# Half-width products in the delta rule's levels, and operand splits moved ahead of three projections, in a one-core fp32 block kernel

## The chip, the cores and the metric

The kernel runs on one core of a Trainium2 chip. The metric is the device time of one execution in microseconds (us), taken as the median of several runs. A core has a matrix engine (PE, with its weight loads shown apart as PEld), a vector engine (DVE), an activation engine (ACT), a general engine (POOL) and a queue engine (SP). In the profile, L532 is line 532 of the kernel.

## The reference, cut to what matters

Two model blocks follow each other over 512 positions of width 2048, in float32. The first ends in a delta rule with 24 value heads, next to a cross attention; its outputs are gated, projected by `w_out` (4096 to 2048) and added to the input. The second block begins with an RMS norm of that sum and one projection whose first tile here holds eight gate columns.

```python
kk = jnp.einsum("bhncd,bhnjd->bhncj", k, k)
m = jnp.where(strict, beta[..., :, None] * kk * decay, 0.0) + jnp.eye(C, dtype=f32)
rhs = jnp.concatenate([v * beta[..., None], k * (beta * jnp.exp(gc))[..., None]], axis=-1)
sol = lax.linalg.triangular_solve(m, rhs, left_side=True, lower=True, unit_diagonal=True)
...
y = jnp.concatenate([mix, xa], axis=-1) * jax.nn.silu(z)
x = x + jnp.einsum("bse,ed->bsd", y, w_out[i])
...
u = rmsnorm(h, norm_w[l])
proj = jnp.einsum('bsd,dc->bsc', u, w_in[l].astype(jnp.float32))
```

## The kernel before, in words

**Projections.** Every weight matrix is a stream of tiles of 2048 x 128. SP loads a tile into `w_raw`, POOL (218 tiles; ACT and DVE do the first 18) splits it into a high part `w_hi` (rounded to fp32r) and the rest `w_lo`. The activations are split the same way into 16 row blocks of `a_hi` (ACT copies) and `a_lo` (DVE subtracts). `gemm` (L386 to L403) issues three matmuls of 512 columns for each of the 16 blocks of a tile: `w_hi` with `a_hi` (L399), `w_hi` with `a_lo` (L400), `w_lo` with `a_hi` (L401). Weights and PSUM have two slots, which the tiles use in turn. A matmul block waits for the semaphore `act_lo` where its operand has only just been split (`fill`).

**Delta rule.** For each of 12 pairs of value heads (index `a`), the 512 positions are four blocks of 128 (index `n`). The triangular inverse of each block grows in levels l = 0 to 6: at level l, a pair of diagonal parts of 2^l columns is joined by one off-diagonal part. Level 0 is a predicated copy alone. At levels 1 to 6 the step `half` computes T1 = N X in bankA (L532), ACT copies bankA to `T1`, and the step `whole` computes the new part of X in bankB (L542, not at the last level) and of its transpose XT in bankC (L544). DVE then writes into X and XT, by `copy_predicated` with the masks `low` and `lowT` (L835), only the elements that the level changes. `NmT`, `X`, `XT` and `T1` are float32, and the trace records each float32 product of the program as two weight loads and two matmuls. `copy_after` and `op` are the helpers by which all DVE instructions go (L835, L829); ACT's go by L1511.

**Order.** `interleave` mixes these steps with the blocks of the tiles of the next pair of heads by a table of weights (`DN_STEPS`). On PE a level is: half(a=0), two gemm blocks, half(a=1), whole(a=0), one gemm block, whole(a=1). All engines walk the same list. `solved` (L551) follows the last level and waits for its copies.

**Around the projection w_out.** Its input has 32 row blocks, handled as two halves of 16. The first 16 tiles (W_OUT + 0 to 15) take the outputs of the first eight head pairs, the next 16 (W_OUT + KT + ...) those of the other four and of the cross attention (`ys`). The outputs lie in DRAM (`y_dram`); `load_early` brings two blocks at a time into a ring of three buffers (`y_rows`), `early_high` and `early_low` split them. `AHEAD` = 4 of the blocks are split before the steps of the last head pair begin, the other 12 are split between these steps, as their gemm block comes up. At the second half, `high(3, ...)` and `fill(3, ...)` split all 16 blocks of `ys` once the last tile of the first half is finished, since `a_hi` and `a_lo` are read until then. The same holds for `high(4, ...)` and `fill(4, ...)` ahead of the gate tile W_GATE. There the norm's sum of squares (`run_sum`, L627) is computed first.

Of the kernel before, what the change touches and what calls it, by code (L numbers as in the profile page):

```python
# [26 lines left out]
P = 128  # L27
T = 512
# [108 lines left out]
AHEAD = 4  # L137
# [26 lines left out]
def build(nc, weights, xT, memT, peT, params, consts, out):  # L164
# [8 lines left out]
    with ctx:  # L173
# [113 lines left out]

        def quad(bank):
            return bank[:, :, :].rearrange("p a (n t) -> p a n t", n=NB)
# [13 lines left out]
        names = ("src_loaded mem_in par_loaded x_made act_hi act_lo squared sq_summed root_ready "  # L303
# [16 lines left out]
        def gains(c, n=1):  # L320
            return par[:, c:c + n]

# [22 lines left out]
        def _(sp):  # L345
# [3 lines left out]
            with sp.Fori(0, (W_END + 1) // 2 - 1) as i:  # L349
                for w in range(2):  # L350
# [3 lines left out]
                        "a p k c -> p (a k) c")).then_inc(raw_loaded[w], 16)  # L354
            for w in range(2):
                sp.wait_ge(raw_loaded[w], 16 * ((W_END + 1) // 2))
# [30 lines left out]
        def _(pe):  # L387
            def gemm(base, c, k, fill=None, i=0, per=0, width=T):
# [13 lines left out]
                if k == KT - 1:  # L402
                    last.then_inc(gemm_done[slot], 1)  # L403

# [93 lines left out]
            def dn_mix(step, j):  # L498
# [25 lines left out]
                elif step[0] == "half":  # L524
# [86 lines left out]
            with pe.Fori(0, (KT - EARLY) // 2) as i:  # L611
                for c in range(2):
                    for k in range(KT):
                        gemm(W_OUT + EARLY, c, k, None, i, 2)
            for k in range(KT):
# [3 lines left out]
            with pe.Fori(0, KT // 2 - 1) as i:  # L619
                for c in range(2):  # L620
                    for k in range(KT):
                        gemm(W_OUT + KT + 2, c, k, None, i, 2)

# [7 lines left out]
            run_sum(2)  # L631
            for k in range(KT):
                gemm(W_GATE, 0, k, 4)

# [188 lines left out]
        def _(v):  # L823
# [189 lines left out]
            def dn_mix(step, j, g=None):  # L1013
# [31 lines left out]
                elif step[0] == "whole":  # L1045
                    l, a = step[1:3]
                    v.wait_ge(s["dd"], level_count(j, l, a))
                    if l < LEVELS - 1:
                        copy_after(v.copy_predicated, X[:, a, :, :], low[:, l:l + 1, :].to_broadcast([P, NB, P]),
                                   quad(bankB)[:, a, :, :])  # L1050
                    copy_after(v.copy_predicated, XT[:, a, :, :], lowT[:, l:l + 1, :].to_broadcast([P, NB, P]),
# [1107 lines left out]
```

## Time and profile before

| what | value |
|---|---|
| median of three runs | 3446.03 us (3445.16 to 3446.71) |
| the profiled execution's own time | 3445.93 us |
| its span, first to last instruction | 3444.1 us |
| mean granted clock of PE | 0.989 of full |
| busy share: PE, PEld | 96%, 80% |
| busy share: DVE, ACT, POOL | 45%, 25%, 49% |

The profile shows one execution. Busy time of PE is the union of overlapping matmuls, so it says that PE had something in flight, and not that each matmul came as fast as it can. The distance from one matmul's start to the next is read from the timeline: a merged row of n equal matmuls is (n - 1) distances and one duration long. Idle time of an engine counts only where PE later waits for it.

### The profile page before, as it was taken

The numbers are of one execution on the slowest core, as the hardware profiler recorded it, in microseconds if no ns is written. First come the engines' busy times: TensorE is split into PE (matmuls) and PEld (weight loads), VectorE is DVE, ScalarE is ACT, GpSimd is POOL, SyncE is SP. The second block draws the span as 40 slices with busy tenths as digits, with TensorE's granted clock in tenths as the row PEclk, the third lists the DMA queues.
The fourth block names the chain that finished last, engine by engine and source line by source line (L and its number), as shares of the span: only waits on it lengthen the run. The fifth ranks groups of instructions, "written<-read, shape, count | busy, mean of one in ns | idle before, by whom it ended". The sixth has DMA issues, their size and how long they took to land.

```text
span 3444.1 us, 47302 instructions
## 1 busy us (share of the span) xinstructions
PE 3302.3 (96%) x17232; PEld 2768.1 (80%) x17232; DVE 1534.9 (45%) x2049; ACT 864.2 (25%) x1291; POOL 1698.4 (49%) x1748
## 2 busy tenths in 40 slices
PE   8999999999999999999899999999998999999996
PEld 7877888888888888888688787777777878778685
DVE  6722245444544454445431213343455665631723
ACT  5411133322332233223310102111113232310411
POOL 0255634433443344334326676656665555556774
PEclk9999999999999999999999999999999999999998
DMA  6322212111211121112214223222223222223222
GB/s 237 125 90 85 95 41 85 61 55 56 84 62 53 57 83 62 54 59 81 97 68 171 86 98 134 94 90 91 97 91 121 76 79 76 88 98 122 74 98 85
DMA packets 53529, 306.51 MB, mean 89 GB/s; under 512 B 5044, under 2 KB 7220, under 8 KB 21716
## 3 DMA queue, kind: packets, MB, share of 16 engines
q1 hardware_dynamic: 33984, 247.48, 21.0%
q10 hardware_dynamic: 19476, 58.05, 4.5%
q8 instruction: 50, 0.82, 0.1%
q14 instruction: 19, 0.16, 0.0%
HBM read 284.74 MB, written 20.77 MB: 89 GB/s over the span
## 4 chain that ended last, share of the span: by engine, by line
PE 82%; DVE 11%; ACT 4%; issue 2%; DMA 1%; ACTq 0%; DVEq 0%
PE gemm_ps L399 19%; PE gemm_ps L401 19%; PE gemm_ps L400 19%; DVE arena L829 9%; PE bankC L544 4%; PE bankB L542 3%; PE bankA L532 3%; ACT arena L1511 2%; PE gemm_ps L746 2%; PE gemm_ps L748 2%; PE gemm_ps L747 2%; PE bankA L702 2%; DVE a_lo L829 1%; ACT a_hi L1511 1%; DVE arena L835 1%
## 5 line engine op out<-in xcount | busy, mean ns | idle before, releaser
L399 PE MATMUL gemm_ps<-a_hi,w_hi 128*128 128x512 f32 (+1 forms) x3472 | 1385.5, 399 | 33.7 <-DVE a_lo L829 28.8
L375 POOL CAST w_hi<-w_raw 128x512 fp32r<-128x512 f32 x872 | 548.6, 671 | 1698.9 <-issue 1541.3
L401 PE MATMUL gemm_ps<-a_hi,w_lo 128*128 128x512 f32 (+1 forms) x3472 | 1332.5, 384 | 0.0
L400 PE MATMUL gemm_ps<-a_lo,w_hi 128*128 128x512 f32 (+1 forms) x3472 | 1330.5, 383 | 0.0
L367 POOL TENSOR_TENSOR w_lo<-w_raw,w_hi 128x512 fp32r<-128x512 f32 x872 | 1153.6, 1354 | 4.2
L399 PEld LDWEIGHTS gemm_ps<-a_hi,w_hi 128*128 128x128 f32 x3472 | 657.6, 189 | 169.2 <-issue 28.2
L401 PEld LDWEIGHTS gemm_ps<-a_hi,w_lo 128*128 128x128 f32 x3472 | 655.7, 189 | 130.9
L400 PEld LDWEIGHTS gemm_ps<-a_lo,w_hi 128*128 128x128 f32 x3472 | 658.0, 190 | 121.7 <-issue 8.4
L829 DVE TENSOR_TENSOR arena<-gemm_ps,arena 128x512 f32<-128x512 f32 (+3 forms) x161 | 107.1, 665 | 633.0 <-PE gemm_ps L401 514.1
L829 DVE RECIPROCAL arena<-arena 128x512 f32<-128x512 f32 (+2 forms) x70 | 172.8, 2468 | 321.3 <-ACT arena L1511 319.1
L1511 ACT ACTIVATE arena<-arena 128x512 f32<-128x512 f32 (+5 forms) x350 | 214.8, 614 | 398.9 <-DVE arena L829 384.5
L829 DVE TENSOR_TENSOR arena<-arena 128x512 f32<-128x512 f32 (+4 forms) x219 | 212.7, 971 | 52.6 <-ACT arena L1801 28.9
L544 PE MATMUL bankC<-arena 128*128 128x128 f32 x1152 | 210.9, 275 | 0.0
L542 PE MATMUL bankB<-arena 128*128 128x128 f32 x960 | 186.1, 275 | 12.3 <-DVE arena L829 12.3
L1511 ACT ACTIVATE arena<-bankA 128x512 f32<-128x512 f32 x144 | 86.1, 598 | 391.6 <-PE bankA L532 391.4
L835 DVE COPY_PREDICATED arena<-con,bankB 128x512 f32<-128x512 uint32 x120 | 88.1, 734 | 202.6 <-PE bankC L544 200.9
L1511 ACT ACT_TABLE_LOAD x104 | 133.4, 1283 | 170.6 <-DVE arena L829 123.5
L544 PEld LDWEIGHTS bankC<-arena 128*128 128x128 f32 x1152 | 170.0, 192 | 1.0
L542 PEld LDWEIGHTS bankB<-arena 128*128 128x128 f32 x960 | 150.0, 191 | 19.3 <-ACT arena L1511 11.9
L829 DVE SCALAR_TENSOR_TENSOR arena<-gemm_ps,arena 128x511 f32<-128x511 f32 x144 | 107.8, 749 | 126.5 <-ACT arena L1511 123.2
L532 PE MATMUL bankA<-arena 128*128 128x128 f32 x1152 | 152.1, 275 | 0.6 <-ACT arena L1511 0.6
L532 PEld LDWEIGHTS bankA<-arena 128*128 128x128 f32 x1152 | 146.2, 191 | 7.5 <-ACT arena L1511 1.0
(162 smaller groups left out, 2679.2 us busy)
## 6 DMA issues: line engine op xcount, KB each, us to landing
w_raw<-w_stream SPq DMA_DIRECT2D x236, 1024.0 KB, 4.9
y_scratch<-arena ACTq DMA_DIRECT2D x20, 512.0 KB, 3.4
arena<-y_scratch ACTq DMA_DIRECT2D x15, 512.0 KB, 4.1
arena<-gc_scratch ACTq DMA_DIRECT2D x12, 512.0 KB, 3.6
arena<-x_t ACTq DMA_DIRECT2D x2, 2048.0 KB, 10.2
arena<-y_scratch ACTq DMA_DIRECT2D x1, 4096.0 KB, 25.2
x_scratch<-arena ACTq DMA_DIRECT2D x1, 4096.0 KB, 12.1
y_out<-arena ACTq DMA_DIRECT2D x4, 1024.0 KB, 3.9
```

The costliest lines, as they stand in the source:

```text
L367: return pool.tensor_tensor(part(w_lo, w, q), part(w_raw, w, q), part(w_hi, w, q).bitcast(F32), ALU.subtract)
L375: pool.tensor_copy(part(w_hi, w, q), part(w_raw, w, q)).then_inc(pool_step, 1)
L399: pe.matmul(o, hi, a_hi[:, k, 0:width], start=(k == 0), stop=False)
L400: pe.matmul(o, hi, a_lo[:, k, 0:width], start=False, stop=False)
L401: last = pe.matmul(o, lo, a_hi[:, k, 0:width], start=False, stop=(k == KT - 1))
L532: last = pe.matmul(quad(bankA)[:, a, n, :], NmT[:, a, n, :], X[:, a, n, :], start=True, stop=True)
L542: pe.matmul(quad(bankB)[:, a, n, :], XT[:, a, n, :], T1[:, a, n, :], start=True, stop=True)
L544: last = pe.matmul(quad(bankC)[:, a, n, :], T1[:, a, n, :], XT[:, a, n, :], start=True, stop=True)
L702: last = pe.matmul(bankA[:, l % 2, b], w[:, b], w[:, b], start=True, stop=True)
L829: d.did(make(*args), sem, value)
L835: d.did(make(*args), sem, value)
L1511: d.did(act.activation(dst, src, func, **kw), sem, value)
```

## The change

The products of a level are issued for 64 of the 128 columns: T1 and the new part of X for the columns of the first half of each pair, the new part of XT for those of the second half. They are written packed into the first 64 columns per block of the PSUM bank (`half_chunk`), and the operand read is strided (`half_columns`). ACT's copy into T1 and DVE's predicated copies handle 256 elements a partition instead of 512. T1 is cleared once before the first head pair.

Ahead of the three projections the splits are moved. `AHEAD` becomes 16: all blocks of the first half are split before the last head pair's steps. The loads of their first four blocks move from ACT's queue to SP's, some tiles earlier. For the second half and for the gate tile, the last tile ahead is taken out of PE's loop and signals each of its blocks by the new semaphore `block_free`; ACT and DVE split block k as soon as that tile has passed it. `run_sum(2)` moves from before the gate tile to after its 13th block.

```diff
-AHEAD = 4
+AHEAD = KT
...
+        def half_chunk(bank, a, n):
+            return bank[:, a, n * (P // 2):(n + 1) * (P // 2)]
...
+        def half_columns(x, l, second):
+            h = 1 << l
+            return x.rearrange("p (b t) -> p b t", t=2 * h)[:, :, h * second:h * second + h]
...
+            asked = W_OUT // 2 - 2
+            with sp.Fori(0, asked) as i:
+                pair_of_tiles(i)
+            sp.wait_ge(s["dy_stored"], 16 * 3)
+            for p in range(2):
+                sp.dma_start(y_rows(p), y_dram[2 * p:2 * p + 2].rearrange("a p t -> p a t")).then_inc(
+                    s[f"early_y{p}"], 16)
...
                     for n in range(NB):
-                        last = pe.matmul(quad(bankA)[:, a, n, :], NmT[:, a, n, :], X[:, a, n, :],
-                                         start=True, stop=True)
+                        last = pe.matmul(half_chunk(bankA, a, n), NmT[:, a, n, :],
+                                         half_columns(X[:, a, n, :], l, 0), start=True, stop=True)
...
-                            pe.matmul(quad(bankB)[:, a, n, :], XT[:, a, n, :], T1[:, a, n, :],
-                                      start=True, stop=True)
-                        last = pe.matmul(quad(bankC)[:, a, n, :], T1[:, a, n, :], XT[:, a, n, :],
-                                         start=True, stop=True)
+                            pe.matmul(half_chunk(bankB, a, n), XT[:, a, n, :],
+                                      half_columns(T1[:, a, n, :], l, 0), start=True, stop=True)
+                        last = pe.matmul(half_chunk(bankC, a, n), T1[:, a, n, :],
+                                         half_columns(XT[:, a, n, :], l, 1), start=True, stop=True)
...
-            pe.wait_ge(s["o_root"], 2 * QKH)
-            run_sum(2)
             for k in range(KT):
                 gemm(W_GATE, 0, k, 4)
+                if k == KT - 4:
+                    run_sum(2)
...
-                        copy_after(v.copy_predicated, X[:, a, :, :], low[:, l:l + 1, :].to_broadcast([P, NB, P]),
-                                   quad(bankB)[:, a, :, :])
+                        copy_after(v.copy_predicated, level_blocks(chunks(X, a), l, 0), level_mask(low, l, 0),
+                                   by_level(half_bank(bankB, a), l))
...
+            add_tile(xt[:, KT - 2, :], W_OUT + KT - 2, 0)
             v.wait_ge(s["ys_loaded"], 16)
-            fill(3, ys, None)
+            for k in range(12):
+                low_block(3, k, ys)
+            add_tile(xt[:, KT - 1, :], W_OUT + KT - 2, 1)
+            for k in range(12, KT):
+                low_block(3, k, ys)
...
-            fill(4, xt, C_NORM2)
+            add_tile(xt[:, KT - 2, :], W_OUT + 2 * KT - 2, 0, q=2, row=KT - 2)
+            for k in range(12):
+                low_block(4, k, xt, C_NORM2)
+            add_tile(xt[:, KT - 1, :], W_OUT + 2 * KT - 2, 1, q=2, row=KT - 1)
+            for k in range(12, KT):
+                low_block(4, k, xt, C_NORM2)
...
-                    op(T1[:, a, :, :], quad(bankA)[:, a, :, :], ACT.Copy, s["t1_sbuf"], level_count(j, l, a))
+                    op(half_columns(chunks(T1, a), l, 0), half_bank(bankA, a).rearrange("p (b t) -> p b t", t=1 << l),
+                       ACT.Copy, s["t1_sbuf"], level_count(j, l, a))
...
+            def high_block(f, base, k, src, gain=None):
+                slot, n = tile_at(base, KT - 1)
+                if k < KT - 1:
+                    act.wait_ge(s["block_free"], (KT - 1) * (f - 3) + k + 1)
+                else:
+                    act.wait_ge(gemm_done[slot], n + 1)
+                op(a_hi[:, k, :], src[:, k, :], ACT.Copy, act_hi, CUT_AT[f] + k + 1,
+                   scale=1.0 if gain is None else gains(gain + k))
```

On DVE, at the start of the last head pair, the rows before are these. `a_lo<-arena,a_hi` is the split of one block; the copy from `con` begins the step `natural`.

```order
L829 TENSOR_TENSOR a_lo<-arena,a_hi 128x512 [waits dy_ready]
L829 TENSOR_TENSOR a_lo<-arena,a_hi 128x512 [waits act_lo,act_hi] x3
L829 COPY arena<-con 128x1024 [waits act_lo]
L829 RECIPROCAL arena<-arena 128x4 [waits dve_step,k_root]
L829 TENSOR_TENSOR arena<-arena 128x8 [waits dve_step] x2
L829 SCALAR_TENSOR_TENSOR arena<-bankA,arena 128x128 [waits dve_step,expd,pair]
L829 SCALAR_TENSOR_TENSOR arena<-bankA,arena 128x128 [waits dve_step] x7
L835 COPY_PREDICATED arena<-con,arena 128x1024 [waits dve_step]
...
L829 TENSOR_TENSOR a_lo<-arena,a_hi 128x512 [waits pm_ready,act_hi]
L829 TENSOR_TENSOR a_lo<-arena,a_hi 128x512 [waits act_lo,act_hi] x11
```

And these are the same place's rows in the changed kernel:

```order
L879 TENSOR_TENSOR a_lo<-arena,a_hi 128x512 [waits dy_ready]
L879 TENSOR_TENSOR a_lo<-arena,a_hi 128x512 [waits act_lo,act_hi] x15
L879 COPY arena<-con 128x1024 [waits act_lo]
L879 RECIPROCAL arena<-arena 128x4 [waits dve_step,k_root]
L879 TENSOR_TENSOR arena<-arena 128x8 [waits dve_step] x2
L879 SCALAR_TENSOR_TENSOR arena<-bankA,arena 128x128 [waits dve_step,expd,pair]
L879 SCALAR_TENSOR_TENSOR arena<-bankA,arena 128x128 [waits dve_step] x7
L885 COPY_PREDICATED arena<-con,arena 128x1024 [waits dve_step]
```

The 12 splits that stood behind the step now stand ahead of it; ACT's list has its 12 copies to `a_hi` moved in the same way.

On DVE, ahead of the gate tile, the rows before are these (the end of the loop over tiles, then the splits, then the norm's reciprocal):

```order
L829 TENSOR_TENSOR arena<-gemm_ps,arena 128x512
L1117 REGISTER_ALU
L829 TENSOR_TENSOR arena<-arena 128x512 [waits evicted0,sq_run]
L1155 REGISTER_ALU
L1155 COMPARE_AND_BRANCH
L95 ISA [waits act_hi,gemm_done1,gemm_done0]
L829 SCALAR_TENSOR_TENSOR a_lo<-arena,par,a_hi 128x512 [waits sq_acc]
L829 SCALAR_TENSOR_TENSOR a_lo<-arena,par,a_hi 128x512 [waits act_lo,act_hi] x15
L829 RECIPROCAL arena<-arena 128x512 [waits act_lo,root_ready]
```

In the changed kernel they are:

```order
L879 TENSOR_TENSOR arena<-gemm_ps,arena 128x512 [waits sq_acc]
L879 TENSOR_TENSOR arena<-arena 128x512 [waits evicted1,sq_run]
L879 SCALAR_TENSOR_TENSOR a_lo<-arena,par,a_hi 128x512 [waits sq_acc,act_hi]
L879 SCALAR_TENSOR_TENSOR a_lo<-arena,par,a_hi 128x512 [waits act_lo,act_hi] x11
L879 TENSOR_TENSOR arena<-gemm_ps,arena 128x512 [waits act_lo,gemm_done0]
L879 TENSOR_TENSOR arena<-arena 128x512 [waits evicted0,sq_run]
L879 SCALAR_TENSOR_TENSOR a_lo<-arena,par,a_hi 128x512 [waits sq_acc,act_hi]
L879 SCALAR_TENSOR_TENSOR a_lo<-arena,par,a_hi 128x512 [waits act_lo,act_hi] x3
L879 RECIPROCAL arena<-arena 128x512 [waits act_lo,root_ready]
```

Twelve of the sixteen splits now stand ahead of the addition that empties the last tile's PSUM slot and of its square; the same pattern, without the square, stands at the second half of `w_out`.

## Rows read from the trace of the kernel before

**Rows 1.** The page: the chain that ended last, by engine.

```profile
PE 82%; DVE 11%; ACT 4%; issue 2%; DMA 1%; ACTq 0%; DVEq 0%
```

**Rows 2.** Groups by form: the levels' products (count, busy us, mean ns).

```profile
L544 PE MATMUL bankC<-arena 128*128 128x128 f32 x1152 | 210.9, 275 | 0.0
L542 PE MATMUL bankB<-arena 128*128 128x128 f32 x960 | 186.1, 275 | 12.3 <-DVE arena L829 12.3
L532 PE MATMUL bankA<-arena 128*128 128x128 f32 x1152 | 152.1, 275 | 0.6 <-ACT arena L1511 0.6
```

**Rows 3.** Timeline of PE (start us, us): products, transposes, transposes of four columns.

```profile
701.18 1.06 PE L532 MATMUL bankA<-arena 128*128 128x128 f32 x8
...
1724.73 1.04 PE L515 MATMUL bankC<-con,arena 128*128 128x128 f32 x8
...
2239.97 0.41 PE L678 MATMUL bankB<-con,arena 4*128 4x4 f32 x4
```

**Rows 4.** Lines L532 and L522 (transposes): duration ns, min/median/max.

```profile
L532 PEld LDWEIGHTS bankA<-arena x1152: 186/192/192, 454.6 to 1781.5; 128*128 128x128 f32 x192
L532 PE MATMUL bankA<-arena x1152: 270/275/377, 454.6 to 1781.6; 128*128 128x128 f32 x192
...
L522 PE MATMUL bankC<-con,arena x96: 272/273/328, 448.9 to 1737.2; 128*128 128x128 f32 x96
```

**Rows 5.** Timeline at the end of a head pair's levels, and a strided form.

```profile
614.46 2.28 PE L551 MATMUL bankA<-arena 128*128 128x128 f32 x16
...
614.80 0.73 DVE L835 COPY_PREDICATED arena<-con,bankC 128x512 f32<-128x512 uint32 x1 [0.85 <-PE bankC L544]
...
L829 DVE TENSOR_TENSOR bankB<-bankC,arena 128x256 f32<-128x256 f32 x48 | 20.8, 432 | 1.6
```

**Rows 6.** Timeline and chain of waits around the last head pair's start.

```profile
1698.50 0.39 PE L508 MATMUL bankA<-arena 128*128 128x128 f32 x2
...
1700.09 3.60 DMA arena<-y_scratch
...
1706.31 0.37 ACTq L1750 DMA_DIRECT2D arena<-y_scratch  x1
...
1707.45 0.69 DVE L829 TENSOR_TENSOR a_lo<-arena,a_hi 128x512 fp32r<-128x512 f32 x1 [0.43 <-ACT a_hi L1511]
...
1712.83 0.63 ACT L1511 ACTIVATE a_hi<-arena 128x512 fp32r<-128x512 f32 x1 [1.32 <-DMA arena<-y_scratch]
...
1713.36 1.29 DVE L835 COPY_PREDICATED arena<-con,arena 128x1024 f32<-128x1024 uint32 x1 [0.16 <-DVE arena L829]
...
1736.47 1.04 PE L522 MATMUL bankC<-con,arena 128*128 128x128 f32 x8
```

**Rows 7.** Timeline of DVE: the tiles' additions around the second half's start.

```profile
1943.51 0.69 DVE L829 TENSOR_TENSOR arena<-gemm_ps,arena 128x512 f32 x1 [10.17 <-PE gemm_ps L401]
...
1962.62 0.69 DVE L829 TENSOR_TENSOR arena<-gemm_ps,arena 128x512 f32<-128x512 f32 x1 [1.07 <-PE gemm_ps L401]
```

**Rows 8.** Groups by form: splits beside POOL's (1947 to 1954) and alone (to 1961.8).

```profile
L829 DVE TENSOR_TENSOR a_lo<-arena,a_hi 128x512 fp32r<-128x512 f32 x5 | 7.3, 1454 | 0.5
...
L367 POOL TENSOR_TENSOR w_lo<-w_raw,w_hi 128x512 fp32r<-128x512 f32 x4 | 6.7, 1709 | 0.0
...
L829 DVE TENSOR_TENSOR a_lo<-arena,a_hi 128x512 fp32r<-128x512 f32 x9 | 6.2, 692 | 1.3 <-DVE a_lo L829 0.5
```

**Rows 9.** Timeline of PE around the gate tile, and after it.

```profile
2125.42 0.39 PE L401 MATMUL gemm_ps<-a_hi,w_lo 128*128 128x512 f32 x1
...
2147.58 0.40 PE L399 MATMUL gemm_ps<-a_hi,w_hi 128*128 128x512 f32 x1
...
2172.86 0.47 PE L399 MATMUL gemm_ps<-a_hi,w_hi 128*128 128x512 f32 x1 [3.34 <-DVE arena L829]
```

**Rows 10.** Stretches: PE busy (instructions), granted clock, DMA share, GB/s.

```profile
1945.00:1955.00 10.00, 6.70 (x21) 1.00 0.09 13
1710.00:1720.00 10.00, 1.91 (x6) 0.63 0.26 88
```

More of the change, by code:

```diff
@@ L321, in gains, with level_mask, by_level, level_blocks @@
             return par[:, c:c + n]
+        def half_columns(x, l, second):
+            h = 1 << l
+            return x.rearrange("p (b t) -> p b t", t=2 * h)[:, :, h * second:h * second + h]
+        def level_mask(mask, l, second):
+            h = 1 << l
+            m = half_columns(mask[:, l, :], l, second)
+            return m[:, None, :, :].to_broadcast([P, NB, P // (2 * h), h])
+        def by_level(x, l):
+            return x.rearrange("p (n b t) -> p n b t", n=NB, t=1 << l)
+        def level_blocks(x, l, second):
+            h = 1 << l
+            return x.rearrange("p (n b t) -> p n b t", n=NB, t=2 * h)[:, :, :, h * second:h * second + h]
+        def chunks(x, a):
+            return x[:, a, :, :].rearrange("p n t -> p (n t)")
         def level_count(j, l, a):
@@ L403, in gemm @@
                     last.then_inc(gemm_done[slot], 1)
+                elif frees:
+                    last.then_inc(s["block_free"], 1)
             def memory_sum(k):
@@ L614, in _ @@
                         gemm(W_OUT + EARLY, c, k, None, i, 2)
+            for c in range(2):
+                for k in range(KT):
+                    gemm(W_OUT + KT - 2, c, k, frees=(c == 1))
             for k in range(KT):
@@ L622, in _ @@
                         gemm(W_OUT + KT + 2, c, k, None, i, 2)
+            for c in range(2):
+                for k in range(KT):
+                    gemm(W_OUT + 2 * KT - 2, c, k, frees=(c == 1))
             def run_sum(q):
@@ L1097, in _ @@
             v.wait_ge(s["y_stored"], 16 * XH)
+            op(v.memset, T1[:, :, :, :], 0.0)
             v.sem_inc(s["o_root"], 2)
@@ L1111, in add_tile @@
                 if q is not None:
-                    add_squares(q, c if per == 0 else 2 * i + 2 + c, c)
+                    add_squares(q, row if row is not None else c if per == 0 else 2 * i + 2 + c, c)
             def add_squares(q, k, c):
@@ L1761, in early_high @@
                     load_early(p + 2)
-            act.wait_ge(s["dy_stored"], 16 * QKH)
-            for p in range(3):
-                if p == 2:
-                    act.wait_ge(s["gate"], QKH)
-                load_early(p)
+            act.wait_ge(s["gate"], QKH)
+            load_early(2)
             for w in range(2):
@@ L1790, in _ @@
             act.wait_ge(s["ys_loaded"], 16)
-            high(3, ys)
+            def high_block(f, base, k, src, gain=None):
+                slot, n = tile_at(base, KT - 1)
+                if k < KT - 1:
+                    act.wait_ge(s["block_free"], (KT - 1) * (f - 3) + k + 1)
+                else:
+                    act.wait_ge(gemm_done[slot], n + 1)
+                op(a_hi[:, k, :], src[:, k, :], ACT.Copy, act_hi, CUT_AT[f] + k + 1,
+                   scale=1.0 if gain is None else gains(gain + k))
+            for k in range(KT):
+                high_block(3, W_OUT, k, ys)
             def run_square(q, k, c):
@@ L1814, in run_squares @@
                         one(2 * i + 2 + c, c, *tile_at(base + 2, c, i, 2))
-                d.leave(KT // 2 - 1)
+                d.leave(KT // 2 - 2)
+                one(KT - 2, 0, *tile_at(base, KT - 2))
+                if q == 2:
+                    for k in range(KT - 2):
+                        high_block(4, W_OUT + KT, k, xt, C_NORM2)
+                one(KT - 1, 1, *tile_at(base, KT - 1))
+                if q == 2:
+                    for k in range(KT - 2, KT):
+                        high_block(4, W_OUT + KT, k, xt, C_NORM2)
             def run_root(q):
@@ L1827, in _ @@
             run_root(2)
-            high(4, xt, gain=C_NORM2)
             act.wait_ge(s["h_lb"], 1)
```

38 lines of the change are left out of this document (25 added, 13 removed).

## The prediction

> **What bounds the kernel now.** I read the page first, then the waits of PE, then the timeline where PE waits. PE is the bound: the chain that ended last runs over it for 82% [rows 1], and the page has it busy 96% of the span. So two questions decide: does a level's product come sooner, and how much of PE's waiting goes. For the first the reader is to look at the distance between products, not at their duration, since they overlap. Eight recorded products of 128 columns take 1.06 us with one duration of 275 ns in it, so one comes every (1060 - 275) / 7 = 112 ns [rows 2 and 3]. For the second, PE has three long waits around the two halves of `w_out` and the gate tile; within the head pairs it hardly waits.
>
> **Products of the levels.** 1152 + 960 + 1152 = 3264 recorded products [rows 2] go from 128 to 64 moving columns. Their weights stay 128 x 128 (`NmT`, `XT`, `T1`). What a product waits for is then the question: its columns, or its weight load.
>
> Columns: transposes move 128 columns too, and come every (1040 - 273) / 7 = 109.6 ns [rows 3 and 4]. The products come every 112 ns, slightly later than the same columns need, so something else already ends last. Loads: a product that finds PE empty takes 377 ns, a transpose that finds it empty 328 ns, at equal columns [rows 4]. The 49 ns are the longer load of a float32 product. Four transposes of only four columns take 0.41 us with one duration of at least 0.2 us in it, about 0.07 us each [rows 3]: with next to nothing to stream, the short load and its overhead set that distance. The long load then sets at most 70 + 49 = 119 ns, and the same sum without the few ns of swapping (61 + 49, from the closest distance that the four allow) gives 110. The observed 112 lies between. I conclude that the products are bound by their weight loads already, and that half the columns bring nothing: 3264 x 0 = 0. Bounds: at best the step falls to 107 ns (3264 x -5 ns = -16 us), at worst two ns are added by the packed writes (+7 us). I take 0, as the row of the products is itself the nearest.
>
> The Trainium skill weighs in on both sides. "TensorE: Matmul & The Clock Gate", section "LDWEIGHTS (loading the stationary operand)", puts a load of P columns at P / 1.2 ns, whatever the moving side does: 107 ns for 128, which speaks against this part of the change; the trace agrees within 5 ns. The same page's "Back-to-back issue gap" prices a lone matmul by its moving columns only; by that rule the step would halve, which is the first rival below.
>
> **ACT's and DVE's copies.** DVE's copies fall from 0.73 us to about 0.43 (a strided form of 256 elements takes 432 ns), ACT's likewise [rows 5]. Nearly all of it lies beside PE. The exception is the end of each head pair: the 16 products of `solved` take 2.28 us, where 15 x 0.112 + 0.275 = 1.95 would do. PE waits for the last copy (start 614.80, 0.73 long) and refills [rows 5]. With a copy of 0.43 us it is done before the first eight products are (614.46 + 0.90 = 615.36). That is 12 x 0.33 = -4 us (bounds -4 and 0). The wait at level 1 of each head pair, 12.3 us in all [rows 2], hangs on DVE's steps ahead of the levels and stays. The clearing of T1 lies beside a tile of PE: 0.
>
> **The first half's splits.** Before: PE ends the products of the last pair's first step at 1698.9 and reaches the transposes of XT at 1736.5 [rows 6]. Between lie 18 gemm blocks and 8 transposes. A tile takes 10.17 + 0.69 = 10.86 us [rows 7], a block 0.68, so that is 12.2 + 0.9 = 13.1 us of work in 37.6: 24.5 us lost. After: SP has loaded four blocks long before, so ACT begins at about 1700.3 and not at 1703.9, as the load's 3.60 us goes from the path [rows 6]. The other 12 blocks come two at a time through three buffers. A buffer is reloaded when DVE has split it, and a load takes 3.6 to 6.5 us (issued 1706.31, used 1712.83 [rows 6]). With about 4.2, and 2.4 for the splits, a pair of blocks comes each 6.6 / 3 = 2.2 us. DVE's first four end near 1706, two of them beside POOL; the last ends at 1706 + 6 x 2.2 = 1719. Then the step `natural`, now queued behind all 16 splits, runs: from the last split to XT's mask copy was 1714.65 - 1708.14 = 6.5 us [rows 6]. PE reaches the transposes at 1725.6: -10.9 us. It has then waited 5 us in front of them, and after such a wait the granted clock fell (0.63 over 1710 to 1720 [rows 10], after an idle of 8 us); I put 2 us for it. Sum: -9. Bounds: -13 if the loads keep to 3.6 us, -4 if each takes 6.5. The two loads that move to SP stand ahead of a weight tile, whose buffer POOL needs only a tile later: 0.
>
> **The second half's splits.** Before, the additions of two neighbouring tiles start at 1943.51 and 1962.62, 19.11 us apart instead of 10.86 [rows 7]: 8.2 us lost. After, DVE starts 1.4 us into the last tile of the first half (one addition, one block of PE). What is late next is DVE itself, as it has now to split beside POOL. A split takes 0.69 us alone and 1.45 beside POOL (mean of five), and POOL's subtractions take 1.71 then, one split to each [rows 8]. POOL is busy 49% of the span for 218 tiles, 7.8 us a tile, and more while DVE is in its way. Going through it instruction by instruction (steps of 1.7 us beside POOL's subtractions, 1.0 beside its casts, 0.8 alone), split 12 ends at 16.5 us, the addition at 17.2, the last split at 23.1. PE wants the last block at 10.9 + 15 x 0.68 = 21.1. So 2 us are lost: -8.2 + 2 = -6. Bounds: -8 (DVE in time), -4 (all at 1.7).
>
> **The gate tile.** From the last matmul ahead (2125.4 + 0.2) to the next tile's first (2147.6) [rows 9] are 21.9 us for a tile of 10.9 and the norm's two products, 0.9: 10.2 lost. After, the same race, with a square and its addition in between for which DVE waits 0.8 us, and splits of 0.86 us alone: split 12 ends at 18.9, split 13 at 23.1, and PE wants block 13 at 19.1. That is a wait of 4 us: -10.2 + 4 = -6. Bounds: -10, and -3 if the clock falls in that wait. The norm's root comes as late as the last split, and DVE's work from there to the wait of 3.34 us at 2172.86 [rows 9] is the same and starts equally late: 0 (-3 to +2).
>
> **Sum.** 0 - 4 - 9 - 6 - 6 = -25 us. The profiled execution took 3445.93 us, span 3444.1 and 1.8 around it, and the median is 3446.03, so nothing has to be shifted: 3421 us. The terms' bounds add up to 3393 and 3443.
>
> **Rivals.**
> *Products bound by their columns.* The load is hidden, and the step goes to half of 107 plus 5 ns, or to the 61 to 70 of the four-column transposes [rows 3]: 3264 x -46 ns = -150 us, in all 3270. For it: the 112 ns lie close to what 128 columns need, and only 2.4 ns separate the two readings. Against: the 49 ns between the two kinds at equal columns [rows 4], which must be on the load's side. Chance 0.07.
> *Strided reads, the side of slower.* PE reads its 64 columns in runs of 2 to 64 elements; before, all its operands are contiguous. If a read in short runs takes four times as long, the step is 213 ns: at all levels 3264 x 101 ns = +330, in all 3750; at level 1 alone (576 products) +58, 3479. It decides from a mean step of 112 + 25 / 3.264 = 120 ns on. For it: no row shows a strided read by PE; DVE reads such runs at full speed (432 ns for 256 elements [rows 5]). Chance 0.05.
> "SBUF — State Buffer", section "Door 1: The DMA port swizzle", of the Trainium skill says that two accesses to a line of 16 bytes suffice for full speed; the shortest run here is two float32. No run here shows it.
> *Clock.* Half as many columns in flight could let the granted clock fall within the levels. Each us at half clock costs half a us, so 50 us of it eat the gain; all levels at half clock would cost 12 x 44 us. Against: from 1945 to 1955, PE ran 21 matmuls of L399 to L401's kind in 10 us, less dense than a level will be, at clock 1.00 [rows 10]. Chance 0.02.
> *The moved splits only trade waits.* DVE and POOL hold each other up more than I reckon, the loads stay at 6.5 us: the lower bounds of all three, 3435. This is inside my own case.
>
> **How the numbers follow.** My case has 0.86. Within it 3405 to 3434 holds most. A run can tell 0.2%, 7 us: of the 0.86, 0.03 fall within it and 0.01 beyond on the slow side. Faster: 0.82 + 0.07 = 0.89. Same 0.03. Slower 0.01 + 0.05 + 0.02 = 0.08. The range 3400 to 3438 leaves out the fast rival, the slow ones and some of each tail.
>
> **What would show it.** Right: merged rows of eight level products with a step of 110 to 113 ns, and durations of about 222 ns (275 less 53); the row of L551's successor at 1.95 us for 16; the head pairs' trips 0.3 us shorter and not 12; the transposes of XT some 11 us earlier; additions at the second half 13 us apart; a wait near block 13 of the gate tile; DVE's splits at 1.5 us and more beside POOL. Wrong: a step near 60 ns (first rival), one above 120 at level 1 (second), granted clock below 1.00 between 455 and 1690 (third), or a DVE copy with short runs above 0.73 us, which PE would wait for at every level.

## The result and the profile after

The changed kernel takes 3466.3 us (median of 4 runs, 3465.6 to 3470.4) against 3446.4 (4 runs, 3445.2 to 3446.8). The ratio is 1.0061, with a 95% interval of 1.0047 to 1.0075: slower by 0.6%, 20 us. Forecast were 3421 us and 3400 to 3438. The profiled execution took 3470.4 us, its span is 3468.6.

The page, read first, shows little of it: PE is busy 96% of the span and holds 83% of the chain, where it held 82% [rows 1]. One figure does point the way: the mean granted clock is 0.976, where it was 0.989. The groups by form answer to [rows 2]:

```profile
L587 PE MATMUL bankC<-arena 128*128 128x64 f32 x1152 | 221.2, 285 | 0.0
L585 PE MATMUL bankB<-arena 128*128 128x64 f32 x960 | 192.7, 284 | 11.0 <-DVE arena L879 10.5 <-ACT arena L1580 0.5
L575 PE MATMUL bankA<-arena 128*128 128x64 f32 x1152 | 160.1, 286 | 1.6 <-ACT arena L1580 1.6
```

Half the columns, and the mean duration rose from 275 to 285 ns. The line of the first product tells why; these are minimum, median and maximum:

```profile
L575 PEld LDWEIGHTS bankA<-arena x1152: 186/192/338, 456.1 to 1818.2; 128*128 128x128 f32 x192
L575 PE MATMUL bankA<-arena x1152: 217/275/421, 456.1 to 1818.3; 128*128 128x64 f32 x192
```

The median stayed; some take 421 ns, and their weight loads 338. The timeline of PE at the second head pair's first levels shows where:

```profile
571.50 1.00 PE L575 MATMUL bankA<-arena 128*128 128x64 f32 x8
572.31 0.48 PE L440 MATMUL gemm_ps<-a_hi,w_hi 128*128 128x512 f32 x1
...
573.78 1.00 PE L575 MATMUL bankA<-arena 128*128 128x64 f32 x8
575.87 0.41 PE L585 MATMUL bankB<-arena 128*128 128x64 f32 x2 [1.09 <-DVE arena L879]
...
583.19 1.91 PE L575 MATMUL bankA<-arena 128*128 128x64 f32 x8
...
587.32 1.00 PE L575 MATMUL bankA<-arena 128*128 128x64 f32 x8
```

Eight products take 1.00 us, then 1.91, then 1.00 again. At full clock the second product of such a row starts 58 ns after the first, where that distance was 108 ns before; it is the one place where fewer columns show. The other six distances are 112 ns, as before: 0.058 + 6 x 0.112 + 0.272 for the last duration = 1.00. The 50 ns do not reach the time either, since the gemm behind starts 0.81 us after the row's start (572.31 - 571.50) as it did before (571.18 - 570.37, below). In the slow row the step is (1.91 - 0.42) / 7 = 213 ns. That is a clock, so the stretches have to be read with the granted clock (length, busy us and instructions of PE, PEld, DVE, ACT, POOL, then the clock). The first and last stretch are the second and seventh pair's, at the same place of their levels, the middle one the sixth pair's:

```profile
576.80:587.00 10.20, 10.20 (x42) 9.52 (x42) 2.92 (x4) 0.38 (x1) 0.00 (x0) 0.50 0.18 74
1054.70:1078.50 23.80, 23.80 (x98) 22.25 (x97) 5.20 (x10) 1.84 (x4) 1.39 (x3) 0.50 0.01 6
1178.80:1189.00 10.20, 10.20 (x81) 9.69 (x81) 3.82 (x6) 0.78 (x2) 0.00 (x0) 1.00 0.17 71
```

Busy share cannot show it: PE is busy 10.20 of 10.20 us in the first and the last, but does 42 instructions in one and 81 in the other. Half clock (1.2 GHz) begins 5 to 7 us after the first level product in eight of twelve pairs and lasts 10.2 us, in one of them 23.9 (the first pair has 3.4 us of it, which cost its trip nothing); in the kernel before no pair's levels have any. The first level products of neighbouring pairs give what it costs:

```profile
690.64 1.00 PE L575 MATMUL bankA<-arena 128*128 128x64 f32 x8
...
1173.50 1.00 PE L575 MATMUL bankA<-arena 128*128 128x64 f32 x8
...
1287.82 1.00 PE L575 MATMUL bankA<-arena 128*128 128x64 f32 x8
```

A trip with the drop takes 690.64 - 571.50 = 119.1 us, one without 1287.82 - 1173.50 = 114.3. So a drop costs 4.8 us, and the long one, of the pair that starts at 1047.94, 11.2 (1173.50 - 1047.94 - 114.3). Before, the trips were 114.65 (685.03 - 570.37):

```profile
570.37 1.05 PE L532 MATMUL bankA<-arena 128*128 128x128 f32 x8
571.18 0.48 PE L399 MATMUL gemm_ps<-a_hi,w_hi 128*128 128x512 f32 x1
...
685.03 1.05 PE L532 MATMUL bankA<-arena 128*128 128x128 f32 x8
```

Both kernels issue the same gemms and products in the same order, up to the norm's two products in the gate tile. So each matmul of one trace can be set against the same of the other, and the lag tells where time went: +1.4 us before the levels, 7 x 4.80 + 11.25 = +44.9 by the clock in the pairs, -3.8 by shorter trips (11 x 0.35), -5.9 in the first half, -6.0 in the second, -5.8 in the gate tile and the tile behind it. The sum is +24.8; the profiled executions differ by 24.5. That is 4 us more than the medians do, as the profiled execution was the slowest of the four.

### The profile page after: what moved, and what is told of

It reads as the page before. It is cut to its first block, busy times and chain, and to the rows that moved or that the text cites. A ratio compares the mean times of both kernels' runs of the same rounds, so it can differ in the third digit from the quotient of the medians.

```text
span 3468.6 us, 47303 instructions
## 1 busy us (share of the span) xinstructions
PE 3343.5 (96%) x17232; PEld 2811.5 (81%) x17232; DVE 1484.1 (43%) x2050; ACT 833.5 (24%) x1291; POOL 1704.9 (49%) x1748
## 4 chain that ended last, share of the span: by engine, by line
PE 83%; DVE 11%; ACT 3%; issue 2%; DMA 1%; ACTq 0%; DVEq 0%
PE gemm_ps L440 19%; PE gemm_ps L442 19%; PE gemm_ps L441 19%; DVE arena L879 8%; PE bankC L587 4%; PE bankA L575 3%; PE bankB L585 3%; PE gemm_ps L796 2%; ACT arena L1580 2%; DVE a_lo L879 2%; PE gemm_ps L798 2%; PE gemm_ps L797 2%; PE bankA L752 2%; PE bankA L594 1%; PE bankB L599 1%
## 5 line engine op out<-in xcount | busy, mean ns | idle before, releaser
L587 PE MATMUL bankC<-arena 128*128 128x64 f32 x1152 | 221.2, 285 | 0.0
L585 PE MATMUL bankB<-arena 128*128 128x64 f32 x960 | 192.7, 284 | 11.0 <-DVE arena L879 10.5
L587 PEld LDWEIGHTS bankC<-arena 128*128 128x128 f32 x1152 | 180.9, 203 | 1.1
L885 DVE COPY_PREDICATED arena<-con,bankB 128x256 f32<-128x256 uint32 x120 | 59.7, 498 | 284.1 <-PE bankC L587 282.7
L585 PEld LDWEIGHTS bankB<-arena 128*128 128x128 f32 x960 | 161.2, 205 | 18.3 <-ACT arena L1580 12.2
L575 PEld LDWEIGHTS bankA<-arena 128*128 128x128 f32 x1152 | 160.1, 207 | 10.0 <-ACT arena L1580 2.0
L1580 ACT ACTIVATE arena<-bankA 128x256 f32<-128x256 f32 x144 | 55.9, 388 | 457.9 <-PE bankA L575 457.8
L575 PE MATMUL bankA<-arena 128*128 128x64 f32 x1152 | 160.1, 286 | 1.6 <-ACT arena L1580 1.6
```

The lines of the kernel that those rows point to most:

```text
L575: last = pe.matmul(half_chunk(bankA, a, n), NmT[:, a, n, :], half_columns(X[:, a, n, :], l, 0), start=True, stop=True)
L585: pe.matmul(half_chunk(bankB, a, n), XT[:, a, n, :], half_columns(T1[:, a, n, :], l, 0), start=True, stop=True)
L587: last = pe.matmul(half_chunk(bankC, a, n), T1[:, a, n, :], half_columns(XT[:, a, n, :], l, 1), start=True, stop=True)
L1580: d.did(act.activation(dst, src, func, **kw), sem, value)
```

## The experiments

The theory to test (A): the 64-column products let the clock fall at the first levels, with the wait of 1.1 us in front of level 1's second products, and all else went about as forecast. The rivals: the moved splits and loads disturb the levels (B); the short runs of columns do, in DVE's and ACT's copies (C) or in PE's reads.

**The change without the levels.** Products and copies as before, splits moved:

```diff
-                        last = pe.matmul(half_chunk(bankA, a, n), NmT[:, a, n, :],
-                                         half_columns(X[:, a, n, :], l, 0), start=True, stop=True)
+                        last = pe.matmul(quad(bankA)[:, a, n, :], NmT[:, a, n, :], X[:, a, n, :],
+                                         start=True, stop=True)
...
```

> The changed kernel with the levels as they were before (products and both kinds of copies over 128 columns, T1 not cleared); only the splits of the two halves of w_out and of the gate tile stay moved. Theory A (the 64-column products let the granted clock fall at each head pair's first levels, and that is all that the change lost): no half clock within the head pairs (456 to 1690 us), trips of 114.6 us, time 3446 - 18 (5.8 + 7.7 + 4.1, what the changed trace gained at the three places) = 3428, perhaps down to 3422 if the half clock after the first half goes too. Theory B (the moved splits and loads disturb the levels): the trips stay at 119.1 us and the time at 3466. Theory C (DVE's and ACT's copies in short runs make the loss): as A for this kernel.

Measured: 3431.0 us, ratio 0.9954 (0.9936 to 0.9971). No half clock in the pairs, trips 114.65. B fell.

**The levels alone**, on the kernel before:

```diff
-                    op(T1[:, a, :, :], quad(bankA)[:, a, :, :], ACT.Copy, s["t1_sbuf"], level_count(j, l, a))
+                    op(half_columns(chunks(T1, a), l, 0), half_bank(bankA, a).rearrange("p (b t) -> p b t", t=1 << l),
+                       ACT.Copy, s["t1_sbuf"], level_count(j, l, a))
...
```

> The kernel before with the level change alone (64-column products, narrowed copies, T1 cleared); splits and loads where they were. Theory A: half clock in most head pairs, 5 to 7 us after the pair's first product; trips of 119 us where it falls and 114.3 where not; time 3446 + 42 = 3488. Theory B: no half clock in the pairs, trips 114.3, time 3443. Theory C: as A for the time, but with gaps in PE's stream instead of a lower clock.

Measured: 3473.7 us (3464 to 3499), ratio 1.007 (1.005 to 1.009). Half clock in eight pairs, as in the changed kernel, in two of them 23.9 us long; trips 119.1 and 114.3. The loss comes with the levels alone. 3488 was too exact: the time varies by 34 us between executions, and the mean granted clock with it, from 0.982 in the fastest to 0.972 in the slowest, which is the one that the trace shows.

**Level 1 wide.** 128 columns in level 1's products only:

```diff
+                        if not (l == 1):
...
+                        else:
+                            last = pe.matmul(quad(bankA)[:, a, n, :], NmT[:, a, n, :], X[:, a, n, :],
+                                             start=True, stop=True)
...
```

> The changed kernel with 128-column products at level 1 alone (their copies stay narrow and read the banks in runs); levels 2 to 6 keep 64 columns. Theory A1 (it is the few columns together with the wait of 1.1 us in front of level 1's second products): no half clock within the pairs, trips of 114.3 us, time 3466 - 42 = 3424. Theory A2 (64 columns alone are too few, at any level): half clock comes at level 2 or 3 of each pair instead, trips stay at 119, time about 3466. The strided-read theory with the shortest runs as the cause would give 3424 too; it is told apart by the contiguous kernel of this call.

Measured: 3427.4 us, ratio 0.9942 (0.9923 to 0.9962), trips 114.3, no half clock in the pairs. The second pair, at the same place as above:

```profile
576.50:586.70 10.20, 10.20 (x82) 9.68 (x80) 3.81 (x6) 0.77 (x2) 0.00 (x0) 1.00 0.17 73
```

Level 2 and the rest run on 64 columns at full clock. So narrow products at levels 2 to 6 are not enough; it needs those of level 1.

**Contiguous columns.**

```diff
-                                         half_columns(X[:, a, n, :], l, 0), start=True, stop=True)
+                                         X[:, a, n, 0:P // 2], start=True, stop=True)
...
```

> The changed kernel whose 64-column products read 64 contiguous columns (the first 64 of X and T1, the last 64 of XT) instead of the columns of their level, so that the levels do not compute the inverse; counts, shapes, weights and all copies are the same. Theory A (width): half clock in the pairs as in the changed kernel, step 112 ns at full clock, time 3466 within 5. Strided-read theory (short runs upset PE's stream or its clock): no half clock, trips 114.3, time 3424.

Measured: 3462.2 us (10 runs, 3448.9 to 3475.4), ratio 1.0047 (1.0030 to 1.0064). Half clock in seven of the pairs, at +5.3 to +6.4 us, trips 119.1 with and 114.3 without. Its second pair:

```profile
576.70:586.90 10.20, 10.20 (x42) 9.52 (x41) 2.92 (x4) 0.38 (x1) 0.00 (x0) 0.50 0.18 74
```

The runs of columns are not the cause; the width is.

**No wait, 64 columns.** If level 1 matters because PE also waits there, filling that wait must keep the clock up:

```diff
-               for s, a, w in (("half", 0, 2), ("half", 1, 0), ("whole", 0, 1), ("whole", 1, 0))]
+               for s, a, w in (("half", 0, 2), ("half", 1, 2 if l == 1 else 0), ("whole", 0, 1), ("whole", 1, 0))]
...
-            + [("head_out", 28)])
+            + [("head_out", 26)])
```

> The changed kernel, 64 columns at every level, with two gemm blocks (1.36 us) moved from the end of each head pair's trip to between the second `half` and the first `whole` of level 1, so that PE has work in place of its wait of 1.1 us for kd_ready. Theory A1 (few columns and the wait together bring the clock down): no half clock in the pairs, trips of 114.3 - 1.1 = 113.2 us, time 3466 - 42 - 12 = 3412. Theory A2 (64 columns are too few by themselves): half clock stays in most pairs, trips near 118, time about 3454.

Measured: 3432.0 us, ratio 0.9955 (0.9942 to 0.9969). No half clock in the pairs but 3.4 us in the first:

```profile
579.30:589.50 10.20, 10.20 (x81) 9.69 (x80) 3.92 (x7) 1.47 (x3) 0.68 (x2) 1.00 0.17 72
```

The cause holds: narrow products and the wait together. (The edit takes the wait away by putting six wide matmuls in its place; which of the two keeps the clock up, no run tells apart.) The 12 us of the wait did not come, trips are 114.8: a wait of 0.9 us a pair has appeared at the last `output` step, and one of 0.3 us at level 3's second `half`. The first of them:

```profile
PE bankC L625 <- DVE arena L879: 10.3, 11, 0.9
```

**Long wait, 128 columns.** The converse:

```diff
-               for s, a, w in (("half", 0, 2), ("half", 1, 0), ("whole", 0, 1), ("whole", 1, 0))]
+               for s, a, w in (("half", 0, 0 if l == 1 else 2), ("half", 1, 0), ("whole", 0, 1), ("whole", 1, 0))]
...
```

> As the kernel with narrow copies and 128-column products, but with the two gemm blocks between level 1's `half` steps moved to the trip's end, so that the wait for kd_ready grows from 1.1 to about 2.4 us. Theory A1 in its sharper form (what counts is the work that the array does in a stretch, whether a wait or narrow products take it away): half clock in the pairs as in the changed kernel, +15 for the wait and about +50 for the clock, 3490. Theory A3 (only narrow products bring the clock down, a wait of a few us does not): no half clock, trips of 115.7 us, time 3427 + 15 = 3442.

Measured: 3462.4 us, ratio 1.0048 (1.0034 to 1.0062). The wait is 2.40 us, and wide products do not always save the clock: it fell in 5 of the 12 pairs, in the first for 6.8 us and in four others for 3.4. The fourth pair:

```profile
816.64 0.46 PE L585 MATMUL bankB<-arena 128*128 128x128 f32 x2 [2.40 <-DVE arena L879]
...
817.61 0.64 PE L585 MATMUL bankB<-arena 128*128 128x128 f32 x2
```

```profile
817.60:821.00 3.40, 3.40 (x15) 3.11 (x14) 1.09 (x2) 0.00 (x0) 0.00 (x0) 0.50 0.51 214
```

Neither of my two times came. Trips are 116.8 us without a drop and 118.4 with one, so a short drop costs 1.6 us. A trip without one was forecast at 115.7; a new wait of 0.9 us a pair makes most of the difference, at the first products of the `rest` steps:

```profile
PE bankA L610 <- DVE arena L879: 9.7, 11, 0.9
```

What the run shows is that the clock can fall at 128 columns too, where the wait is longer, and that it then comes back sooner than with narrow products behind it (3.4 us against 10.2). It does not show that the wait alone does it: the edit also takes two gemm blocks, six wide matmuls, out of the stretch ahead.

**Narrow copies, wide products.**

```diff
-                                   by_level(half_bank(bankB, a), l))
+                                   level_blocks(bankB[:, a, :], l, 0))
...
```

> The changed kernel with all products over 128 columns again; ACT's and DVE's copies stay narrow and pick their columns out of the whole banks. Theory A: no half clock in the pairs, trips of 114.3 us, time 3431 (moved splits alone) - 4 = 3427, as much as the kernel with only level 1 wide; so 64 columns bring nothing at levels 2 to 6 either. Rival (the 64-column products of levels 2 to 6 do save PE time, hidden in the changed kernel by the clock): trips and time come out above those of the kernel with level 1 wide, by more than 3 us in all.

Measured: 3425.3 us, ratio 0.9942 (0.9928 to 0.9955), trips 114.35. The kernel with 64 columns at levels 2 to 6 has 114.3: the narrow products save nothing worth having, even without a drop.

**The same with the wait filled.** Two blocks from the trip's end:

```diff
-               for s, a, w in (("half", 0, 2), ("half", 1, 0), ("whole", 0, 1), ("whole", 1, 0))]
+               for s, a, w in (("half", 0, 2), ("half", 1, 2 if l == 1 else 0), ("whole", 0, 1), ("whole", 1, 0))]
...
-            + [("head_out", 28)])
+            + [("head_out", 26)])
```

> As the kernel with narrow copies and 128-column products, with two gemm blocks moved from each trip's end to the place of the wait for kd_ready at level 1. Every theory: trips of 113.2 us, time 3427 - 12 = 3415, unless head_out at the trip's end then comes too late for the next trip and gives some of it back (up to 3427).

Measured: 3430.7 us, ratio 0.9953 (0.9939 to 0.9966), trips 114.9. A miss: the wait is gone, and the same 0.9 us at `output` and the 0.3 us at level 3's second `half` are there. One block instead of two:

```diff
+               for s, a, w in (("half", 0, 2), ("half", 1, 1 if l == 1 else 0), ("whole", 0, 1), ("whole", 1, 0))]
...
+            + [("head_out", 27)])
```

> As the kernel with narrow copies and 128-column products (3425), with one gemm block (0.68 us) moved from each trip's end to the place of the wait for kd_ready at level 1, where two blocks only traded that wait for one of 0.9 us at the last `output` step (trips of 114.9 us). Theory 1 (the later wait appears once the levels end more than 0.45 us later than before): 0.4 us left of the first wait, 0.25 us of the later one, trips of 114.0 us, time 3422. Theory 2 (any delay of the levels comes back in full at the trip's end): trips of 114.6 us, 3428.

Measured: 3440.7 us (11 runs), ratio 0.9982 (0.9973 to 0.9991), trips 115.5. A worse miss: both theories took the later wait for a question of amounts. It has grown to 1.6 us, because of what now stands ahead on DVE:

```profile
988.47 2.32 DVE L879 SCALAR_TENSOR_TENSOR arena<-gemm_ps,arena 128x511 f32<-128x511 f32 x3 [2.40 <-ACT arena L1580]
990.82 0.74 DVE L879 SCALAR_TENSOR_TENSOR arena<-bankA,arena 128x128 f32<-128x128 f32 x2
```

```profile
991.61 0.71 PE L625 MATMUL bankC<-arena 128*128 128x128 f32 x4 [1.62 <-DVE arena L879]
```

In the kernel that the block was taken from, the operand for PE came first and the tile's eviction after it:

```profile
979.81 0.74 DVE L879 SCALAR_TENSOR_TENSOR arena<-bankA,arena 128x128 f32<-128x128 f32 x2 [2.13 <-PE bankA L610]
981.76 2.32 DVE L879 SCALAR_TENSOR_TENSOR arena<-gemm_ps,arena 128x511 f32<-128x511 f32 x3 [1.21 <-ACT arena L1580]
```

Taking blocks from the trip's end moves `output` past the end of a tile, and DVE evicts that tile before it makes the operand for which PE waits. So the block has to come from a place between the levels and `output`:

```diff
-               for s, a, w in (("half", 0, 2), ("half", 1, 0), ("whole", 0, 1), ("whole", 1, 0))]
-            + [("solved", 6)]
+               for s, a, w in (("half", 0, 2), ("half", 1, 1 if l == 1 else 0), ("whole", 0, 1), ("whole", 1, 0))]
+            + [("solved", 5)]
```

> As the kernel with narrow copies and 128-column products (3425), with one gemm block moved from behind the `solved` step to the place of the wait for kd_ready at level 1. Nothing after `solved` comes later against the tile's blocks than before, and DVE's instructions stand in the same order as in that kernel, so no eviction comes ahead of what the `output` steps need. 0.4 us of the wait stays: trips of 114.35 - 0.68 = 113.7 us, time 3425 - 7.5 = 3418. If instead the step `rest` behind `solved` has to wait for DVE by what was taken from it, trips of 114.3 and 3425.

Measured: 3418.0 us (3416.6 to 3419.7), ratio 0.9914 (0.9901 to 0.9928). Trips 113.64, and the wait left is 0.29 us:

```profile
575.15 0.46 PE L585 MATMUL bankB<-arena 128*128 128x128 f32 x2 [0.29 <-DVE arena L879]
```

This is the kernel with the lowest median of the study, 29 us below the kernel before. Two blocks from the same place:

```diff
+               for s, a, w in (("half", 0, 2), ("half", 1, 2 if l == 1 else 0), ("whole", 0, 1), ("whole", 1, 0))]
+            + [("solved", 4)]
```

> The same with two blocks: the whole wait of 1.1 us is covered, but DVE's eviction of a tile comes ahead of two of its level copies. Trips of 113.3 us and 3413 if only the wait counts; 113.7 and 3418 if the levels lose 0.4 us again, as in the first kernel with two blocks; 114.3 and above if `rest` waits.

Measured: 3423.4 us (3412.5 to 3426.0), ratio 0.9920 (0.9905 to 0.9935), trips 113.66. The middle case in its trips: the wait for `kd_ready` is gone, but one of 0.3 us has come at level 3's second `half`, and the levels take 44.7 us from first product to `solved` where they took 44.0. The second block buys nothing.

**The first half alone**, on the kernel before:

```diff
-AHEAD = 4
+AHEAD = KT
...
-            act.wait_ge(s["dy_stored"], 16 * QKH)
-            for p in range(3):
-                if p == 2:
-                    act.wait_ge(s["gate"], QKH)
-                load_early(p)
+            act.wait_ge(s["gate"], QKH)
+            load_early(2)
```

> The kernel before with the first half's splits alone moved (all 16 ahead of the last head pair's `natural` step, two loads given to SP, AHEAD = 16). The trace of the kernel with all moved splits and no level change has the stretch from the last `natural` product to the last pair's first level product 5.7 us shorter than before, where -9 was forecast. Theory 1 (the term is what that trace shows): 37.1 us instead of 42.8 in that stretch, time 3446.5 - 5.7 = 3441. Theory 2 (the first half brings the forecast's 9, and the other moved splits, by what POOL and the queues do, took some of it): 3437.

Measured: 3445.6 us (11 runs), ratio 0.9999 (0.9990 to 1.0008). Neither: no gain to be measured. Yet against the same matmuls before, its profiled execution gains 5.6 us in the stretch. The rest of the trace gives them back: 1.3 us ahead of the levels, and 4.5 in three places that the edit does not touch: 1.0 near 2175, 3.0 near 2240 and 0.4 near 2605. At the first two more half clock falls than before. The two in this kernel, and below in the kernel before:

```profile
2160.00:2180.00 20.00, 16.68 (x63) 13.21 (x62) 8.35 (x13) 0.63 (x1) 10.55 (x10) 0.83 0.30 106
2235.00:2250.00 15.00, 12.28 (x46) 9.10 (x46) 11.13 (x17) 4.19 (x6) 8.48 (x8) 0.77 0.35 131
```

```profile
2160.00:2180.00 20.00, 16.66 (x67) 13.29 (x66) 12.75 (x16) 1.89 (x2) 15.05 (x14) 0.91 0.21 65
2235.00:2250.00 15.00, 12.28 (x60) 9.64 (x59) 8.76 (x11) 4.20 (x6) 10.23 (x10) 1.00 0.25 75
```

PE is as busy in both and does fewer instructions. Other kernels of this study have such stretches at 2215 to 2290 too; in the kernel with the splits alone one of 6.8 us, at 2226, cost 2.9 us of its profiled execution; it took 3431 us where 3428 were expected. I did not try to find out what decides between a kernel that has one and a kernel that has none.

## Why the prediction was wrong

The step that failed is the rival "Clock", with its 0.02, and in it the sentence "Against: from 1945 to 1955, PE ran 21 matmuls of L399 to L401's kind in 10 us, less dense than a level will be, at clock 1.00 [rows 10]". It counted instructions. Those 21 move 512 columns each; a level product of the changed kernel moves 64, only 6 of the 31 matmuls in the stretch ahead of a drop are gemms, and PE waits 1.1 us in it. No row of before had narrow products beside a wait, so rows 10 spoke of another kind of work. So the sum has no term for the clock within the pairs, where the trace has +44.9 us. The mechanism as I wrote it ("50 us of it eat the gain") was the right one: the eight pairs had 96 us of half clock (7 x 10.24 + 23.9), and it cost 44.9. The kernels with level 1 wide (3427) and with all products wide (3425) show what is left without this rival, 4 to 6 us above the forecast; 3 us of it are the term of the first half.

Point by point:

- Products 0: right. The step is 112 ns at 64 columns at full clock, at every level, with runs of 2 columns as with 64. That refutes both rivals on the step, columns-bound (3270) and strided reads (3479 and up). The durations were wrong, at no cost: 222 ns were forecast, the median stayed 275, and of the products of L575 only those right behind a gemm have some 220. That the weight load is what holds the others to 112 ns is the reading that fits; the runs show that the columns do not. The Trainium skill's rule for a weight load ("TensorE: Matmul & The Clock Gate", section "LDWEIGHTS (loading the stationary operand)": 128 columns divided by 1.2, 107 ns) agrees with that step within 5 ns. It speaks of one time whatever the clock; the trace has 213 ns at half clock, so if the load sets the step, it slows with the clock.
- `solved` -4: right, -3.8. The row that answers to [rows 5] has 2.00 us where there were 2.28, and DVE's last copy 0.45 where there were 0.73:

```profile
620.37 2.00 PE L594 MATMUL bankA<-arena 128*128 128x128 f32 x16
```

```profile
620.71 0.45 DVE L885 COPY_PREDICATED arena<-con,bankC 128x256 f32<-128x256 uint32 x1 [1.14 <-PE bankC L587]
```

- `copy_predicated` with about 0.43 us: right from level 2 on, wrong at level 1, where the runs are two elements long. There a copy of 256 elements takes 0.73 us, as long as one of 512 took before. Nothing waits for it, so it cost no time. Level 1 and level 2 of the seventh pair:

```profile
1182.50 0.73 DVE L885 COPY_PREDICATED arena<-con,bankB 128x256 f32<-128x256 uint32 x1 [0.80 <-PE bankC L587]
...
1187.45 0.43 DVE L885 COPY_PREDICATED arena<-con,bankB 128x256 f32<-128x256 uint32 x1 [3.33 <-PE bankC L587]
```

- First half -9: too much, -5.9. From the start of the last product of `natural` (1741.2) PE reached the transposes of XT after 30.3 us, where 27.0 were forecast (before 37.9): -7.6 instead of -10.9. Half clock behind them took 1.7 back, where 2 were put. DVE's last split ended 23 us after that product, not 20, since the loads through three buffers took longer, and the mask copy 7.1 us after that, not 6.5. PE waited three times, 3.4, 3.2 and 4.7 us, where I had named one, of 5:

```profile
1744.87 0.77 PE L440 MATMUL gemm_ps<-a_hi,w_hi 128*128 128x512 f32 x1 [3.44 <-DVE a_lo L879]
...
1757.03 0.50 PE L440 MATMUL gemm_ps<-a_hi,w_hi 128*128 128x512 f32 x1 [3.18 <-DVE a_lo L879]
...
1771.47 1.97 PE L565 MATMUL bankC<-con,arena 128*128 128x128 f32 x8 [4.73 <-DVE arena L885]
```

```profile
1755.62 0.63 ACT L1580 ACTIVATE a_hi<-arena 128x512 fp32r<-128x512 f32 x1 [3.63 <-DMA arena<-y_scratch]
```

- Second half -6: right, -6.0. The rows that answer to [rows 7 and 8] show six splits beside POOL in 8.78 us, 1.46 each as before, and PE's waits at the last blocks, 2 x 0.73 us:

```profile
1970.31 8.78 DVE L879 TENSOR_TENSOR a_lo<-arena,a_hi 128x512 fp32r<-128x512 f32 x6 [0.67 <-ACT a_hi L1580]
```

- Gate tile -6: right, -5.8 (-5.0 in the tile, and -0.8 since the wait of 3.34 us behind it [rows 9] is 2.53 now), with a wait of 2.8 us near block 13, where 4 were forecast:

```profile
2167.71 0.80 PE L440 MATMUL gemm_ps<-a_hi,w_hi 128*128 128x512 f32 x1 [2.79 <-DVE a_lo L879]
```

- "The wait at level 1 stays": right, 1.09 us, but I gave it no weight. It is the other half of the cause.

The list of what would show the clock rival ("granted clock below 1.00 between 455 and 1690") was there. What was missing is a look at that rival with the rows of the level itself: its wait and its share of gemms.

## What to carry to other kernels

Where the step of a stream of products does not follow its columns (112 ns with 128 and with 64 here), fewer moving columns save no time, and beside a wait of PE they cost 44.9 us of clock. Leave such products wide, narrow only the copies behind them, and look for waits of the tensor engine in stretches of small products: filling such a wait is worth at most its own length, and it may keep the clock up. When blocks are moved to fill it, check what passes the end of a tile on the other engines: one block from behind `solved` gave 7 us, one from the trip's end cost 15.

## What the hardware showed that I had not expected

- PE's busy share does not tell whether the clock will fall. From the second pair's first level product PE is busy 4.11 of 5.20 us in the changed kernel and 4.18 of 5.20 in the kernel before, each with 31 matmuls and one wait, of 1.1 and 1.0 us; behind the first the clock fell, behind the second not:

```profile
571.50:576.70 5.20, 4.11 (x31) 3.74 (x29) 4.33 (x4) 0.81 (x2) 2.85 (x2) 1.00 0.21 50
```

```profile
570.40:575.60 5.20, 4.18 (x31) 3.76 (x30) 4.28 (x4) 1.20 (x2) 2.80 (x2) 1.00 0.24 47
```

  The Trainium skill ("TensorE: Matmul & The Clock Gate", section "HAM oscillation — how this bites in real kernels") puts such falls down to long waits of PE for a DMA. Here the wait is 1.1 us, for DVE, and the clock fell beside it with products of 64 columns and not with 128.

- The drop begins 0.35 us later against the first product from pair to pair (5.27, 5.59, 5.96, 6.32, 6.69 us), the last of these is the long one, and the next pair has none. The same program had 3449 to 3475 us in ten runs (contiguous columns), 26 us or some five drops of 4.8, and a mean granted clock of 0.983 in the fastest and 0.975 in the slowest. So the amount of half clock is not fixed by the program; that it is whole drops in the pairs that come and go, the one trace does not show.
- PE reads runs of two float32 at its full step of 112 ns. DVE's predicated copy of 256 elements does not: it takes 0.73 us with runs of two, as long as one of 512 elements in a piece, and 0.44 us with runs of 4 to 64. The mean of all, 0.49 us, hides this. Why runs of two are slow was not looked into.
